# The down product of two feed-forwards as seven half-size products

## The reference, cut to what matters

```python
def swiglu(h, w_gu, w_down):
    gu = h @ w_gu                      # [512, 1024] @ [1024, 5632]
    g, u = jnp.split(gu, 2, axis=-1)
    return (jax.nn.silu(g) * u) @ w_down    # [512, 2816] @ [2816, 1024]
...
x = x + mixer_or_attention(...)
x = x + swiglu(rms_norm_2(x, ffn_norm[l]), w_gu[l], w_down[l])
...
return rms_norm_2(x, final_norm)
```

## Time and profile before

| | us |
|---|---|
| median of three runs (2000.58 to 2003.66) | 2002.74 |
| span of the profiled execution | 1994.7 |
| TensorE busy in it | 1939.8 |
| VectorE busy | 1178.0 |
| ScalarE busy | 977.8 |
| mean granted TensorE clock, share of full speed | 0.998 |
| first feed-forward, end of its last matmul | 1374.2 |
| second feed-forward, matmuls from and to | 1626.2, 1985.5 |

### The profile page before, as it was taken

One profiled execution on the slowest core, in us unless ns is written; L12 is line 12 of the kernel. 1 busy time (PEld: TensorE's weight loads), 2 busy tenths in 40 slices (PEclk: granted clock), 3 DMA queues, 4 the chain that ended last, 5 costly groups with the idle time before them and its releaser, 6 DMA issues.

```text
span 1994.7 us, 23044 instructions
## 1 busy us (share of the span) xinstructions
PE 1939.8 (97%) x8950; PEld 1559.6 (78%) x8950; DVE 1178.0 (59%) x1544; ACT 977.8 (49%) x1522; POOL 202.7 (10%) x273
## 2 busy tenths in 40 slices
PE   5999999999999999999999999999999999999998
PEld 4768768888888888668788888887777778888886
DVE  6777699899999999663443333335445453333323
ACT  4533268888888888553243222124455542222221
POOL 3200211131211110020010000001011110000001
PEclk9999999999999999999999999999999999999999
DMA  8564589999999999942322323223212142323201
GB/s 297 173 214 170 180 295 364 369 376 374 374 372 371 358 369 362 350 128 81 106 82 89 104 85 105 95 74 105 67 43 85 43 136 86 106 86 105 95 32 42
DMA packets 200024, 366.49 MB, mean 184 GB/s; under 512 B 13514, under 2 KB 84055, under 8 KB 199914
## 3 DMA queue, kind: packets, MB, share of 16 engines
q1 hardware_dynamic: 181152, 343.20, 49.1%
q10 hardware_dynamic: 8714, 11.17, 1.6%
q0 software_dynamic: 10048, 10.62, 1.6%
HBM read 365.05 MB, written 24.65 MB: 195 GB/s over the span
## 4 chain that ended last, share of the span: by engine, by line
PE 83%; DVE 7%; DMA 4%; ACT 2%; issue 2%; POOL 1%; ACTq 0%; POOLq 0%; DVEq 0%
PE ps L288 80%; DVE wlo L235 3%; DMA raw<-in_w_expert_gate 3%; ACT whi L216 1%; PE ps L2215 1%; DMA VR<-in_b_subln 1%; PE ps L2242 1%; DVE XT0l L2298 0%; PE ps L2907 0%; ACT YB L2307 0%; ACT whi L220 0%; DVE acc L285 0%; PE ps L790 0%; DVE hT4l L856 0%; DMA raw<-in_ada_w 0%
## 5 line engine op out<-in xcount | busy, mean ns | idle before, releaser
L235 DVE TENSOR_TENSOR wlo<-raw,whi 128x1024 fp32r<-128x1024 f32 x574 | 671.1, 1214 | 295.0 <-ACT whi L216 292.3
L216 ACT ACTIVATE whi<-raw 128x1024 fp32r<-128x1024 f32 x574 | 571.5, 1048 | 214.2 <-PE ps L288 191.1
L288 PE MATMUL ps<-hT5h,whi 128*128 128x512 f32 x352 | 137.0, 389 | 0.6 <-DVE hT5l L285 0.6
L288 PE MATMUL ps<-hT3h,whi 128*128 128x512 f32 x352 | 137.0, 389 | 0.6 <-DVE hT3l L285 0.6
L288 PE MATMUL ps<-hT5l,whi 128*128 128x512 f32 x352 | 136.9, 389 | 0.0
L288 PE MATMUL ps<-hT3h,wlo 128*128 128x512 f32 x352 | 136.9, 389 | 0.0
L288 PE MATMUL ps<-hT5h,wlo 128*128 128x512 f32 x352 | 136.9, 389 | 0.0
L288 PE MATMUL ps<-hT3l,whi 128*128 128x512 f32 x352 | 136.9, 389 | 0.0
L2770 DVE TENSOR_TENSOR tmpT<-tmpT,ps 128x512 f32<-128x512 f32 x44 | 30.1, 684 | 139.3 <-PE ps L288 139.3
L288 PE MATMUL ps<-whi,XT1h 128*128 128x512 f32 x256 | 102.7, 401 | 1.5 <-DVE XT1l L2298 1.5
L288 PE MATMUL ps<-whi,XT0h 128*128 128x512 f32 x256 | 102.7, 401 | 1.1 <-DVE XT0l L2298 1.1
(11 more groups left out here) (475 smaller groups left out, 4102.4 us busy)
## 6 DMA issues: line engine op xcount, KB each, us to landing
raw<-in_w_expert_gate SPq DMA_DIRECT2D x64, 1024.0 KB
raw<-in_w_expert_up SPq DMA_DIRECT2D x64, 1024.0 KB
raw<-in_w_expert_down SPq DMA_DIRECT2D x64, 1024.0 KB
raw<-in_ffn_w_gu SPq DMA_DIRECT2D x44, 1024.0 KB
raw<-in_ffn_w_down SPq DMA_DIRECT2D x20, 1024.0 KB
raw<-in_ada_w SPq DMA_DIRECT2D x24, 512.0 KB, 5.0
raw<-in_a_w_in SPq DMA_DIRECT2D x8, 1024.0 KB
raw<-in_kv_w SPq DMA_DIRECT2D x8, 1024.0 KB
```

The source lines that it names most:

```text
L216: e.activation(hi[:, c], raw[:, c], ACT.Copy).then_inc(self.S("w_hi"), 1)
L235: e.tensor_tensor(lo[:, c], raw[:, c], hi[:, c].bitcast(F32), ALU.subtract).then_inc(self.S("w_lo"), 1)
L288: return e.matmul(o, l, r, start=start, stop=stop, skip_group_check=True)
```

## The change: what it does

The down product of each group is cut in halves: tokens (0 to 255 and 256 to 511), features of the group (the first 4, 4 or 3 blocks of 128, and the rest) and output columns (0 to 511 and 512 to 1023). In place of the eight products of halves there are seven, by Strassen's scheme in Winograd's form. With A for the activations, kept in fp32 in `FA` (the space of `XN`), and B for the weights, the products are, by their numbers in the code:

- 1: A11 B11; 2: A12 B21; 3: S4 B22; 4: A22 T4; 5: S1 T1; 6: S2 T2; 7: S3 T3
- S1 = A21 + A22, S2 = S1 - A11, S4 = A12 - S2, S3 = A22 - S2 (five subtractions or additions on VectorE for a group, since S1 is made in two parts)
- T1 = B12 - B11, T2 = B22 - T1, T3 = T2 - B11, T4 = B21 - T2 (`quad_sum`, two instructions each on VectorE)

A product is two blocks of 128 tokens by 4, 4 or 3 feature blocks by three matmuls: 24 or 18 matmuls of 128x512 (`ORDER` gives the order 1, 5, 6, 3, 7, 2, 4, in the group of six 1, 5, 6, 3, 2, 7, 4). Products 1, 6, 7 and 4 add up in the same pair of banks, and 5 and 3 in another: after each product VectorE adds the state of the banks to the part of `X` that needs it (`ADDS`), and the next product on that bank waits for it (`R.claim`). The left operand of each product is split when its sum is there (`high` and `low` in `ffn_act` and `ffn_vec`), no longer once for all.

Around it: `whi` and `wlo` have three places in a feed-forward in place of four, the fourth holds two of the group's four blocks of weights (`raw4`, `raw5`); gate and up units use two `raw` buffers; in `ffn_vec` the low parts are asked for with `W.low(e, j + 1)`, where j is the pair's up unit; of `vv` only the first block is split ahead of attention; the squares of the rows go in another order (`rows_act`).

```diff
+ORDER = [(1, 5, 6, 3, 7, 2, 4), (1, 5, 6, 3, 7, 2, 4), (1, 5, 6, 3, 2, 7, 4)]
+ADDS = {1: (0, 0), 5: (2, 1), 6: (0, 1), 3: (0, 1), 7: (2, 1), 2: (0, 0), 4: (2, 0)}
...
+        (first, over, low, right), a, made = self.quads[q]
+        n = a * 256
+        b11, b12, b21, b22 = ([self.raw[self.raw_of[i][0]][:, h * n:(h + 1) * n] for h in range(2)]
+                              for i in (first, over, low, right))
+        out_, x, y, landed = {1: (b12, b12, b11, (first, over)), 2: (self.sum, b22, b12, (right,)),
+                              3: (b11, self.sum, b11, ()), 4: (b12, b21, self.sum, (low,))}[t]
...
+        for h in range(2):
+            m = e.tensor_tensor(out_[h][:, 0:n], x[h][:, 0:n], y[h][:, 0:n], ALU.subtract)
+        m.then_inc(self.S("quad_sum"), 1)
...
+            held = W.place_last[3]
+            W.places = [0, 1, 2]
...
+                def unit(i, m):
+                    n0 = (f0 + 2 * i) * P + (DFF if m == "fu" else 0)
+                    pairs.append((f"{m}{l}", W.item(up[:, :, n0:n0 + 256], len(pairs) % 2)))
+                def block(k, h, place):
+                    quad.append(W.item(down[:, f0 + k:f0 + k + a, h:h + 512], place))
...
+            W.places = [0, 1, 2, 3]
+            W.place_last[3] = W.index[f"fd{l}"][-7 + ORDER[-1].index(2)]
...
+                for p in order:
+                    name = f"fd{l}.{f0}.{p}"
+                    R.plan(name, 2, V_, on=collections.deque(v if p in (5, 3) else y if p == 2 else z))
+                    W.ends[W.index[f"fd{l}"][nd]] = R.full(name, 1)
+                    nd += 1
+                R.turn.extend(v + y + z)
...
+            def product(gi, f0, a, m, p):
+                k = 7 * (gi % 3) + m
+                j = W.index[f"fd{l}"][k]
+                w, x = W.parts(j), [operand(AT, i, k, a) for i in range(2)]
+                for tb in range(2):
+                    b = R.claim(e, f"fd{l}.{f0}.{p}", tb)
+                    for kc in range(a):
+                        if tb == 0 and kc in (0, a - 2):
+                            e.wait_ge(*W.half(j, 0 if kc == 0 else 1))
+                            if kc == 0 or m == 1:
+                                e.wait_ge(S("left_lo"), splits(gi, m, 0 if m == 1 and kc == 0 else 1))
+                        i = mm3(e, b[:, :], [y[:, kc, tb * P:(tb + 1) * P] for y in x], [y[:, kc, :] for y in w],
+                                kc == 0 and p in (1, 5, 2), kc == a - 1)
+                    i.then_inc(*R.fill(f"fd{l}.{f0}.{p}", tb))
...
+                for m in range(2, 7):
+                    W.high(e, js[m] + 1)
+                    if m < 5 and ORDER[gi % 3][m] in (6, 3, 7):
+                        e.wait_ge(S("s_sum"), 5 * gi + {6: 3, 3: 4, 7: 5}[ORDER[gi % 3][m]])
+                    elif ORDER[gi % 3][m] == 7:
+                        e.wait_ge(S("s_sum"), 5 * gi + 5)
+                    high(gi, f0, a, m)
+                if f0 + fn == 22:
+                    W.high(e, js[6] + 2)
...
+            def low(gi, a, m, lo=0, hi=None):
+                k, p = 7 * (gi % 3) + m, ORDER[gi % 3][m]
+                cs = slice(lo, a if hi is None else hi)
+                e.wait_ge(S("left_hi"), splits(gi, m, 0 if hi is not None else 1))
+                e.tensor_tensor(operand(AT, 1, k, a)[:, cs, :], left(p, a)[:, cs, :], operand(AT, 0, k, a)[:, cs, :].bitcast(F32),
+                                ALU.subtract).then_inc(S("left_lo"), 1)
+            def add(f0, p, tb):
+                t0, h = ADDS[p]
+                x = X[:, t0 + tb, h * 512:(h + 1) * 512]
+                e.wait_ge(*R.full(f"fd{l}.{f0}.{p}", tb))
+                if p in (3, 7, 2):
+                    e.wait_ge(*R.done(f"fd{l}.{f0}.{({3: 6, 7: 5, 2: 1})[p]}", tb))
+                e.tensor_tensor(x, x, R.bank(f"fd{l}.{f0}.{p}", tb)[:, :], ALU.add).then_inc(*R.free(f"fd{l}.{f0}.{p}", tb))
...
                 for f in range(0, fn, 2):
-                    for m in ("fg", "fu"):
-                        j = W.index[f"{m}{l}"][ng]
-                        W.low(e, j + W.depth(j))
+                    j = W.index[f"fu{l}"][ng]
+                    W.low(e, j + 1)
+                    if f == fn - 2:
+                        W.low(e, js[0] + 1)
+                    if f == 4:
+                        low(gi, a, 0)
+                    if f == fn - 2:
+                        low(gi, a, 1, 0, a - 2)
+                        W.quad_sum(e, gi, 2)
+                        W.quad_sum(e, gi, 3)
+                        W.low(e, js[1] + 1)
+                        W.quad_sum(e, gi, 4)
                     for k in range(2):
                         e.wait_ge(*R.done(f"fg{l}.{ng}", k))
                         e.wait_ge(*R.full(f"fu{l}.{ng}", k))
-                        e.tensor_tensor(tmpT[k][:, :], tmpT[k][:, :], R.bank(f"fu{l}.{ng}", k)[:, :], ALU.mult).then_inc(
+                        e.tensor_tensor(FA[:, f + k, :], FA[:, f + k, :], R.bank(f"fu{l}.{ng}", k)[:, :], ALU.mult).then_inc(
                             *R.free(f"fu{l}.{ng}", k))
-                        e.wait_ge(S("a_hi"), 22 * l + f0 + f + k + 1)
-                        e.tensor_tensor(AT[1][:, f + k, :], tmpT[k][:, :], AT[0][:, f + k, :].bitcast(F32),
-                                        ALU.subtract).then_inc(S("a_lo"), 1)
+                    e.wait_ge(*R.done(f"fu{l}.{ng}", 1))
                     ng += 1
-                for h in range(2):
-                    for j in W.index[f"fd{l}"][nd:nd + 2]:
-                        W.low(e, min(j + W.depth(j), LATE[l]))
-                    add_vec(e, [(f"fd{l}.{f0}.{h}", tb) for tb in range(TB)], h, then if f0 + fn == 22 and h == 1 else None, True)
-                    nd += 2
+                    if f == fn - 4:
+                        cs = slice(0, a - 2)
+                        e.tensor_tensor(a21[:, cs, :], a21[:, cs, :], a22[:, cs, :], ALU.add).then_inc(S("s_sum"), 1)
+                        W.quad_sum(e, gi, 1)
+                cs = slice(a - 2, a)
+                e.tensor_tensor(a21[:, cs, :], a21[:, cs, :], a22[:, cs, :], ALU.add).then_inc(S("s_sum"), 1)
+                low(gi, a, 1, a - 2)
+                e.wait_ge(S("left_lo"), splits(gi, 1))
+                e.tensor_tensor(a21, a21, a11, ALU.subtract).then_inc(S("s_sum"), 1)
+                W.low(e, js[2] + 1)
+                low(gi, a, 2)
+                for tb in range(2):
+                    add(f0, 1, tb)
+                e.wait_ge(S("left_lo"), splits(gi, 2))
+                e.tensor_tensor(a11, a12, a21, ALU.subtract).then_inc(S("s_sum"), 1)
+                W.low(e, js[3] + 1)
+                low(gi, a, 3)
+                e.wait_ge(S("s_sum"), 5 * gi + 4)
+                e.tensor_tensor(a21, a22, a21, ALU.subtract).then_inc(S("s_sum"), 1)
+                for m in range(4, 7):
+                    for tb in range(2):
+                        add(f0, order[m - 3], tb)
+                    W.low(e, js[m] + 1)
+                    low(gi, a, m)
+                if f0 + fn < 22:
+                    for m in (4, 5, 6):
+                        for tb in range(2):
+                            add(f0, order[m], tb)
+                        if m < 6:
+                            W.low(e, js[m] + 4)
+                else:
+                    add(f0, order[4], 0)
+                    add(f0, order[4], 1)
+                    W.low(e, js[6] + 2)
+                    add(f0, order[5], 0)
+                    then(0)
+                    add(f0, order[5], 1)
+                    then(1)
+                    add(f0, order[6], 0)
+                    then(2)
+                    add(f0, order[6], 1)
+                    then(3)
```

More of the change, by code:

```diff
@@ L147, in add, with quad @@
         self.place_last[place] = j
[L148 removed]
+        self.w.append((i, a, b))
         self.gain.append(gain)
[L150 removed]
+        self.after.append(after)
+        if i is not None:
+            self.done_by[i] = j
+        return j
+    def add(self, name, ap, a, b, gain=None):
+        self.split(name, self.item(ap), a, b, gain)
+    def quad(self, name, items, a, order):
+        q = len(self.quads)
+        made = {}
+        first, over, low, right = items
+        of = {1: (first, None), 5: (over, 1), 6: (None, 2), 3: (right, None), 7: (first, 3), 2: (low, None), 4: (over, 4)}
+        for p in order:
+            i, t = of[p]
+            made[p] = self.split(name, i, a, 512, after=None if t is None else (self.S("quad_sum"), 4 * q + t))
+        self.quads.append((items, a, made))
+        return q
     def depth(self, j):
```

234 lines of the change are left out of this document (147 added, 87 removed).

## The result

The changed kernel is slower: 2069.27 us median of four runs (2067.33 to 2078.14), against 2002.76 for the kernel before; the estimated ratio is 1.0353, 95% interval 1.0334 to 1.0373 (the two medians alone give 1.033). The forecast was 2038.8 with a range up to 2055, so the sign was right and the size was not: about 30 us are missing from it. The profiled execution has a span of 2067.6 us, 72.9 more than before, where the sum said 36.0. By spans 36.9 us are missing. The two differ because the forecast set the median 8.0 above the span, as it was for the kernel before, and here it is 1.7 above.

The account below looks back on a forecast made before the run. TensorE was taken to bound the kernel, busy 1939.8 of 1994.7 us. 52.7 + 5.7 + 3.4 + 4.1 - 29.9 = 36.0 us more gave a span of 2030.7, with 8.0 added a forecast of 2038.8 us, range 2028 to 2055.

Parts of the forecast that it names:

- The products: Down products of both feed-forwards: 132 fewer matmuls at 0.2268 us each, 29.9 us less.
- The wait at each gate unit: TensorE waits for late low parts: nine waits of 2.46, four of 5.36, two of 4.57; 52.7 us more.
- T: The moment at which TensorE would go on to the next gate unit if it did not have to wait.
- The seven products: Waits for VectorE within the down products: none in groups of eight, some at products 3 and 4 otherwise; 5.7 us more.
- rival 2: Seven products wait because VectorE's half-token layout instructions cost up to twice: 34 us more, 2073; chance 0.08.
- The ends: Feed-forward ends: last addition stands behind block 2's scaling; 2.4 us in the second, 1.0 in the first, 3.4 in sum.
- Attention's start: Second block of value weights split late: 5.0 us at the 13th matmul, a wait of 0.84 goes; net 4.1 us more.
- Rival 1: The clock falls after seven long TensorE stops, 1.7 us each: 12 us more, time 2051; chance 0.20.

Follow-up runs that it names:

- e1: Changed kernel with the low parts of the next gate and up units made ahead of the multiplications, except in a group's last pair; ratio 0.9999 to before.
- e7: e6 with value weights loaded into the units' buffers and split in pieces, product 7's additions and the last addition moved ahead; 1976.72 us, ratio 0.9883 to before.
- e6: e1 with the second feed-forward's first up unit split later and banks exchanged in the first feed-forward's last group; ratio 0.9938 to before.
- e2: Changed kernel with 9 to 22 useless matmuls filling TensorE's waits at gate units; ratio 1.0244 to before.
- e3: Changed kernel with the last pair's gate-unit low part ahead of the sums for S1 and T1, making all 15 stops short; ratio 1.0200 to before.
- e4: Kernel before, its down product unchanged, with only the next unit's low part moved behind the current pair's multiplications; ratio 1.0440 to before.
- e8: Changed kernel with the edit of e2 and the second feed-forward's first up unit split later; ratio 1.0180 to before, span 2033.1 us.

## Why the prediction failed, step by step

**The products, 29.9 us less: right.** 8818 matmuls, and e1 and e7 show the gain once nothing stops.

**The wait at each gate unit: right to a tenth.** A wait of 2.46 counted from T is an idle time of 2.46 - 0.11 (the longer first matmul) - 0.16 (the modelled end behind T) = 2.19 in a row; measured 2.20. For 5.36 and 4.57 that is 5.09 and 4.30; measured 5.08 and 4.27. Nine, four and two of them, as counted. (Its lower bound of 47.5 for the sum is 48.2 by its own figures, which changes nothing.)

**The seven products: right.** No stop in a group of eight. The addition for S1 is in the half-token layout and takes 0.69 us for 512 elements (the row at 1224.25 above), as the plain rows do, so rival 2 is out. Product 3 in the group of six stops for 0.46, which costs 0.7 (0.8 forecast), in both feed-forwards; product 4 in the first stops for 3.24, which costs 3.5 (3.2), and in the second for two short waits, at its first and its tenth matmul, of 0.3 and 0.4 (0.9). The sum is 5.7, as forecast. The first of these in TensorE's timeline, 0.44 behind the start of the matmul before it, where 0.23 is the step of the others:

```profile
2051.12 0.50 PE L349 MATMUL ps<-whi,AT5h 128*128 128x512 f32 x1
```

One reason was wrong although the sum was not: I held the data of `vv` to be in time. ScalarE waited 4.22 us for it, until 1390.71, 4.9 us after its issue at 1385.80, where I had counted 4.3.

**The ends: right in size.** 2.5 against 2.4 in the second feed-forward. The parts as I wrote them (0.61, 1.7 and 1.28 behind an end 2.04 earlier) make only 1.6; the rest is that block 2's addition is late itself, at 2054.85, behind the scaling of block 1. In the first, what I had put at 1.0 is mixed with the next.

**Attention's start: right in size by luck.** I had 5.0 at the 13th matmul and missed the bank, whose 3.90 came first and covered it. e6 shows the two to be alternatives. With the passage ahead of it 5.9 us were measured where 5.1 stood in the sum: 3.5 more of wait and 1.0 for the end of the first feed-forward, and in attention itself 1.4, which is the clock behind the stop (5.0 us at half, 2.5) less the wait of 0.8 that went as forecast.

**Rival 1, the clock: this is the step that failed.** The sum has no term for the clock. I made it a rival with a chance of 0.20 and a size of 12 us; it was the case and cost 21.5 behind the gate units (e2), in the two feed-forwards together. Two sub-steps were mis-sized. I priced a fall at 1.7 us, the one at 241 us; that holds behind the stops of 2.2 and 4.3 us, but behind the four of 5.1 it is 3.1. And "I hold the short waits of 2.5 to be safe" rested on one row, the stop of 2.33 at 966.01 that left the clock at 1.00. It was one case of a thing that happens in some: 10 of 24 stops of 2.2 us were followed by a fall, 4 of them among the nine of the changed kernel. By the traces this is 4 x 3.1 + 6 x 1.7 = 22.6 us, beside the 21.5 of e2. The very stop that I took for proof, in code that the change leaves alone, is followed by a fall in the changed kernel's own trace:

```profile
964.89 0.68 PE L349 MATMUL ps<-whi,hT2h 128*128 128x512 f32 x1 [2.33 <-DVE hT2l L2798]
...
965.00:968.00 3.00, 3.00 (x8) 2.32 (x9) 3.00 (x6) 3.00 (x5) 0.00 (x0) 0.50 0.02 5
```

The Trainium skill, "TensorE: Matmul & The Clock Gate", section on HAM oscillation, says that waits between bursts of matmuls bring the clock down again and again; the traces agree, with 31 falls at the 47 stops for a low part of weights (15 in the changed kernel, 15 in e3, 17 in e4).

**The passage to the second feed-forward: not in the sum at all.** "Around it: `whi` and `wlo` have three places" was read for the feed-forwards alone. This is the second step that failed, a term of 12.8 us put at nothing. It comes from a block that another stage's code splits ahead for a feed-forward, into a place whose last reader had changed. It is neither a removed, added nor moved instruction, so the look at what moved could not find it; the list with its buffer numbers would have.

So of the 36.9 us that the span lies above the sum, 21.5 are the clock behind the gate units and 12.8 the place. The rest of 2.6 is 0.5 ahead of the first feed-forward, 1.2 in the two feed-forwards (the clock behind product 4's stop is in it), 0.8 around attention's start and 0.1 at the end.

## What to carry to other kernels

When a change takes away a buffer, go through every place where another stage fills or claims one in that rotation, and compare buffer and bank numbers, not only the order. Ask for the operand of the next unit ahead of any instruction that waits for the current one; a late one costs the wait and, in 31 of 47 cases here, a clock at half behind it. And price a stop of TensorE of over 2 us as more than its length, here 1.3 to 1.5 times (36.9 and some 10 us where all 15 are short, in e3; 52.7 and 21.5 in the changed kernel; 85.9 for 59.3 in e4), or fill it.

## What the runs showed of the hardware

At the stops for a low part of weights the granted clock fell to 0.50 in 10 of 24 cases of 2.2 us (the changed kernel and e3), in 15 of 17 of 3.4 us (e4), and in all 6 of 4.3 and 5.1 us (the changed kernel). The stretch at 0.50 lasts some 3.5 us, and nearly 7 with the stops of 5.1 us, where it begins 0.7 to 0.8 us ahead of the stop's end. That part costs nothing, which is one reason why the loss in time (21.5 us) is less than what the clock's rows add up to (a mean of 0.96 and 0.97 over 385 and 383 us is 27, and the fall at product 4 is in it). Behind one and the same stop of 2.33 us the clock stayed at 1.00 in the kernel before (at 966.01) and fell in the changed one (at 964.89); what decides between the two is not shown here. With 9 to 22 matmuls of no use in the stops at the gate units, it did not fall at any of the 15 in e2, nor in e8.
